# Delta-rule order, output projection and weight splits of a diffusion backbone: four edits in one change

## The reference

```
def odd_mixer(h_lat, h_ctx, ...):
    p = h @ w_in                      # q, k, v, z, a, b
    q, k, v = silu(short_conv(qkv));  q, k = l2_normalize(...)
    # per chunk: m = strict(kb k^T * decay); T = (I + m)^-1
    # u = T vb; w = T (kb exp(gcum))
    # scan over chunks, forward and backward: v_new = u - w S
    #   o = (q exp(g)) S + (q k^T * decay) v_new;  S = S exp(g_last) + ...
    o = rms_norm(o, norm_g) * silu(z)
    return o @ w_out                  # latent tokens only
```

## Time and profile before

| | |
|---|---|
| median of 3 runs | 1341.44 us (1340.7 to 1342.94) |
| profiled execution | 1340.64 us, span 1338.9 us |
| busy PE, DVE, ACT, POOL | 1200.1, 608.9, 567.1, 128.4 us |
| chain that ended last | PE 83%, DVE 6%, ACT 5%, issue 2%, DMA 2% |
| granted PE clock, mean | 0.947 of full |

### The profile page before, as it was taken

The page is one execution under the profiler, slowest core; times in us unless marked ns, Lnnn a source line. Parts: engine busy times, 40 slices in busy tenths (PEclk is TensorE's granted clock), DMA queues, the critical chain, the costliest instruction groups (busy, mean ns, idle before and its releaser), DMA issues.

```text
span 1338.9 us, 18940 instructions
## 1 busy us (share of the span) xinstructions
PE 1200.1 (90%) x7669; PEld 967.4 (72%) x7669; DVE 608.9 (45%) x948; ACT 567.1 (42%) x1028; POOL 128.4 (10%) x118
## 2 busy tenths in 40 slices
PE   5599999999889999999999698786988977999996
PEld 3377744457568888888887387664878967999996
DVE  2432247662543333332222663458756545554444
ACT  2432245663462223223222656253373636544442
POOL 0020320100001111110000000010015130111000
PEclk9699989999889999999999899887979987999998
DMA  8555558893223333333333032122203022666660
GB/s 287 181 166 164 172 178 299 279 264 83 63 63 95 95 95 96 101 97 88 99 89 97 16 95 53 42 63 68 75 2 96 1 77 81 189 187 178 176 184 33
DMA packets 239396, 159.62 MB, mean 119 GB/s; under 512 B 14779, under 2 KB 213837, under 8 KB 239309
## 3 DMA queue, kind: packets, MB, share of 16 engines
q1 hardware_dynamic: 238528, 158.11, 40.3%
q10 hardware_dynamic: 780, 0.29, 0.1%
HBM read 157.33 MB, written 1.05 MB: 118 GB/s over the span
## 4 chain that ended last, share of the span: by engine, by line
PE 83%; DVE 6%; ACT 5%; issue 2%; DMA 2%; POOL 1%; ACTq 0%; DVEq 0%; POOLq 0%
PE bank L1335 56%; PE bank L1373 4%; PE bank L1362 4%; PE bank L1322 3%; PE bank L1391 2%; PE bank L1484 2%; PE bank L1494 1%; PE bank L742 1%; PE bank L1515 1%; DVE v_conv L1070 1%; PE bank L745 1%; PE bank L1381 1%; PE bank L1510 1%; DMA alog_row<-in_gdn_a_log 1%; PE bank L699 1%
## 5 line engine op out<-in xcount | busy, mean ns | idle before, releaser
L1335 PE MATMUL bank<-h_hi,w_hi 128*128 128x512 f32 (+1 forms) x1048 | 374.4, 357 | 11.7 <-issue 11.7
L1335 PE MATMUL bank<-h_lo,w_hi 128*128 128x512 f32 (+1 forms) x1048 | 369.6, 353 | 0.0
L1335 PE MATMUL bank<-h_hi,w_lo 128*128 128x512 f32 (+1 forms) x1048 | 369.5, 353 | 0.0
L1781 DVE TENSOR_TENSOR w_lo<-w_raw,w_hi 128x1024 fp32r<-128x1024 f32 (+1 forms) x187 | 229.9, 1232 | 298.7 <-ACT w_hi L1577 298.5
L1577 ACT ACTIVATE w_hi<-w_raw 128x1024 fp32r<-128x1024 f32 (+1 forms) x187 | 192.7, 1036 | 98.4 <-PE bank L1335 82.3
L1335 PEld LDWEIGHTS bank<-h_hi,w_hi 128*128 128x128 f32 x1048 | 201.6, 192 | 39.5 <-issue 13.4
L1335 PEld LDWEIGHTS bank<-h_hi,w_lo 128*128 128x128 f32 x1048 | 201.3, 192 | 26.4
L1335 PEld LDWEIGHTS bank<-h_lo,w_hi 128*128 128x128 f32 x1048 | 201.3, 192 | 25.9 <-issue 0.5
L1335 PE MATMUL bank<-act_hi,w_hi 128*128 128x512 f32 (+1 forms) x352 | 118.3, 336 | 0.0
L1335 PE MATMUL bank<-act_lo,w_hi 128*128 128x512 f32 (+1 forms) x352 | 118.3, 336 | 0.0
L1335 PE MATMUL bank<-act_hi,w_lo 128*128 128x512 f32 (+1 forms) x352 | 118.3, 336 | 0.0
(11 more groups left out here) (260 smaller groups left out, 1448.6 us busy)
## 6 DMA issues: line engine op xcount, KB each, us to landing
w_raw<-in_ada_w SPq DMA_DIRECT2D x96, 512.0 KB, 5.2
w_raw<-in_ffn_w_gate_up SPq DMA_DIRECT2D x88, 512.0 KB, 3.8
w_raw<-in_ffn_w_down SPq DMA_DIRECT2D x32, 512.0 KB, 3.9
w_raw<-in_gdn_w_in SPq DMA_DIRECT2D x32, 512.0 KB, 4.0
w_raw<-in_attn_w_in SPq DMA_DIRECT2D x14, 512.0 KB, 4.0
w_raw<-in_ffn_w_down SPq DMA_DIRECT2D x16, 384.0 KB, 3.4
w_raw<-in_gdn_w_out SPq DMA_DIRECT2D x8, 512.0 KB, 5.4
w_raw<-in_attn_w_in SPq DMA_DIRECT2D x8, 256.0 KB, 3.5
```

What stands on the lines that cost most here:

```text
L1335: m = nc.tensor.matmul(dst, stationary(a, k), moving(b, k), start=(first and k == kk[0] and a == b == 0), stop=(last and k == kk[-1] and a ...
L1781: nc.vector.tensor_tensor(w_lo[where[key] % N_RAW][:, 0:tiles, 0:w], raw_slot(key)[:, 0:tiles, 0:w], w_hi[m % N_SPLIT][:, 0:tiles, 0:w].bi ...
```

## The change

1. Eight modulation chunks, not four, ahead of the first norm's sums.
2. Every norm: two weight tiles are split ahead of it, the third inside the loop over tiles, behind tile five.
3. The delta rule: decay banks 4 a step (before 3, 3, 4, 6); SiLU of k one step earlier; on DVE the Gram banks of the last step stand ahead of the taps of the tile; the second block transpose is moved behind `h_whole`; the 30 inversion steps lie evenly over steps 17 to 29, and the inverses leave one step later.
4. The output projection of the delta rule: plain fp32 with raw weights, the first three tiles interleaved over k; DVE gates and scales into `o_whole`. The splits and POOL's share are gone. Each read follows the O groups of its head half. The next feed-forward's three tiles are split during output tiles 5 to 7.

```diff
-ADA_FIRST = 4
+ADA_FIRST = 8
...
-        E_AT = {5: E_BANKS[0:3], 6: E_BANKS[3:6], 7: E_BANKS[6:10], 8: E_BANKS[10:16]}
+        E_AT = {5 + m: E_BANKS[4 * m:4 * m + 4] for m in range(4)}
...
+def split_out(split_to, i, m):
+    if i == 0:
+        split_to(ahead(("attout", m)))
+    elif m >= 5:
+        split_to(split_no[FIRST_CHUNK[3]] + m - 5)
...
-            jobs += scan_jobs(3, None, ("KS", "VN", "O"))
-            return jobs + [("read", pair) for pair in range(READS)]
+            jobs += scan_jobs(3, None, ("KS", "VN"))
+            for hq in range(2):
+                jobs += [("O", 3, d, hq) for d in range(2)] + [("read", 2 * hq + m) for m in range(2)]
+            return jobs
...
     for n in range(LAST + 1):        # gdn_vector
         if n < WHOLE_AT:
             split_to(ahead(("gdn",) + GDN_STEPS[n], LAST_SPLIT))
+        if n - 1 in G_AT:
+            gram_banks(n - 1)
...
-                if n == 15:
+                if n == 16:
                     link(blocks_out(1))
                     block_scale(1).then_inc(blocks_in, 1)
...
+            def project_gdn_out():
+                tiles = 3
+                dsts = [take(("y", 2, m))[:, CTX:T] for m in range(tiles)]
+                for m in range(tiles):
+                    wait_raw(pe, ("gdnout", m))
+                for k in range(KT):
+                    pe.wait_ge(o_whole_ready, k // 2 + 1)
+                    for m in range(tiles):
+                        ins = nc.tensor.matmul(dsts[m], raw_slot(("gdnout", m))[:, k, :], o_whole[:, k, :],
+                                               start=(k == 0), stop=(k == KT - 1))
...
             def pre_norm(i):         # DVE; ACT has the same behind its k == KT - 3
                 lo = first_token(i)
-                if i:
-                    split_to(ahead(FIRST_CHUNK[i]))
+                split_to(split_no[FIRST_CHUNK[i]] + 1)
...
+                        if m == KT - 4:
+                            split_to(ahead(FIRST_CHUNK[i]))
```

More of the change, by code:

```diff
@@ L377, in backbone @@
         where = {key: n for n, key in enumerate(chunks)}
-        split_chunks = [key for key in chunks if key[0] != "ada" and not (key[0] == "gdn" and key[1] in "qz")]
+        split_chunks = [key for key in chunks if key[0] != "ada" and key[0] != "gdnout"
+                        and not (key[0] == "gdn" and key[1] in "qz")]
         split_no = {key: n for n, key in enumerate(split_chunks)}
@@ L449, in backbone @@
         E_BANKS = [(c, d, hq) for c in range(CHUNKS) for d, hq in GROUPS]
-        E_AT = {5: E_BANKS[0:3], 6: E_BANKS[3:6], 7: E_BANKS[6:10], 8: E_BANKS[10:16]}
[L451 to L454, removed]
+        E_AT = {5 + m: E_BANKS[4 * m:4 * m + 4] for m in range(4)}
+        SOLVE_AT = {}
+        for m in range(13):
+            SOLVE_AT[17 + m] = [j for j in range(1, BLOCK - 1) if (j - 1) * 13 // 30 == m]
         VT_AT = {18 + m: [2 * m, 2 * m + 1] for m in range(GH // 2)}
@@ L1374, in project_whole @@
                 finish(m, key)
+            def project_gdn_out():
[8 more added lines that the diff above has]
+                                               start=(k == 0), stop=(k == KT - 1))
+                        if k == KT - 1:
+                            finish(ins, ("y", 2, m))
+                for m in range(tiles, KT):
+                    dst = take(("y", 2, m))[:, CTX:T]
+                    wait_raw(pe, ("gdnout", m))
+                    for k in range(KT):
+                        ins = nc.tensor.matmul(dst, raw_slot(("gdnout", m))[:, k, :], o_whole[:, k, :], start=(k == 0),
+                                               stop=(k == KT - 1))
+                    finish(ins, ("y", 2, m))
             def to_tokens(job, src, ring="work"):
@@ L1639, in out_project @@
                 for m in range(KT):
-                    split_to(ahead((name, m)))
+                    split_out(split_to, i, m)
                     take_y(i, m)
@@ L1893, in _ @@
             ada(ada_after("start", 0))
-            split_to(ahead(FIRST_CHUNK[0]))
             pre_norm(0)
@@ L1974, in _ @@
             for m in range(KT):
-                split_to(ahead(("attout", m)))
+                split_out(split_to, 0, m)
                 sum_y(0, m)
@@ L1984, in _ @@
                 for m in range(KT):
-                    split_to(ahead(("gdnout", m)))
+                    split_out(split_to, 2, m)
                     sum_y(2, m)
```

95 lines of the change are left out of this document (40 added, 55 removed).

## The result

The changed kernel takes 1300.19 us, the median of four runs (1297.48 to 1302.44), against 1342.19 for the kernel before beside it: a ratio of 0.9685, 95% interval 0.9661 to 0.9709, so 42.0 us less. Measured again later it had 0.9692 (0.9668 to 0.9717). The forecast was 1304.7 within 1298 to 1315. The profiled execution took 1299.38 us with a span of 1297.6 and a granted clock of 0.965, 41.3 us under that of before.

What follows compares the result with a forecast made beforehand. PE's long row of three-pass matmuls was taken as the floor, with gains only where it is broken: start -9.0, norms +0.1, delta rule to the join -21.9, scan and projection -5.9, sum -36.7, time 1304.7 us, range 1298 to 1315.

Steps and rivals of the forecast that it cites:

- The start: First projection: no hole in the load queue and no third tile ahead, so h_work begins at 42.9, not 51.92: -9.0 us.
- The third split: All norms: moved behind tile five it delays the last h_lo tiles, mostly hidden by PE's lag: +0.1 us, bounds 0 and +2.
- The delta rule's tiles: Delta rule up to h_whole: Gram multiplies run beside the tile; rebuilt stretch brings h_whole to 889.0 from 912.20: -23.2 us.
- The give-back at the join: End of q and z tiles: inverses leave a step later, giving back 1.3 us, bounds 0 and +4; -21.9 remains.
- the first still starts cold: First q tile behind h_whole: still begins on a low clock, 30 matmuls in 9.63 us at 0.50.
- rival (d): Q and z tiles: clock stays down, sixteen tiles and turns run at 1.2 GHz, +61 us, time 1365.7; chance 0.02.
- Scan and projection: End of scan: w_lo gone, projection starts 8.6 us sooner but costs 2.7 more: -5.9 us, bounds -3 and -7.
- My estimate of 33 us by that page: Output projection: fp32 counted as four passes, not three, turns 25.02 into some 33 us; gain nearly nothing, sum -31.
- The sum: Whole kernel: -9.0 + 0.1 - 21.9 - 5.9 = -36.7 us, giving 1304.7; chance of this forecast 0.65.
- (a): Start: loads 16 and 17 come after a queue hole, only the third tile's -3.8 is won, time 1309.9; chance 0.11.
- (b): Delta rule: DVE becomes the bound and the inverse slips by two tiles of 3.46, time 1311.6; chance 0.11.
- (c): Delta rule: Gram wait moved, not removed; one 4 us wait stays with 1.7 of cold clock, 1310.4; chance 0.08.

Runs made afterwards that it cites:

- both start edits: Kernel before with eight modulation chunks ahead of the first norm and the third split behind tile five of each norm: 1334.35 us, ratio 0.9947.
- the two dealings: Changed kernel with decay banks 4, 4, 4, 4 over steps 5 to 8 (1298.91 us, 0.9692) and with the old 3, 3, 4, 6 (1299.74 us, 0.9692).
- mask later: Kernel before with one added wait, so POOL masks the blocks only when h_whole is done: 1339.8 us, ratio 0.9993.
- norms late: Changed kernel with ACT's key norms at step 16 instead of 14: 1296.24 us, ratio 0.9666.
- the projection alone: Kernel before with the fp32 output projection and its read-outs (change 4) and none of the other changes: 1332.91 us, ratio 0.9945.

## Why the prediction was right, step by step

**The start** (-9.0): right as a sum, -8.97 in the profiled pair. Part of that is chance: the kernels without an edit here start anywhere from 54.0 to 56.1, and both edits together are worth some 8. The bound for the third tile alone (-3.8) measured -3.8 against their mean of 54.95. Inside the sum two terms were off and cancelled. The second weight tile's last byte came 2 us later than I had it in both kernels (ACT starts its split at 45.07 before, where I had 43.1, and at 40.44 after, where I had 38.5), and the work behind it is 2.5 to 3.0 us and not 4.4 to 5.0. What I had only as 0.6 us off that work is an edge of its own, the modulation: DVE finishes its fold at 40.68, and only then splits both tiles. The 38.2 that the Trainium skill's page "DMA: Bandwidth & Descriptors" would give was further off still from the 40.44.

**The third split** (+0.1, bounds 0 and +2): mis-sized. Norm 2 takes 36.4 us on the mean of seven traces with it (35.8 to 36.6) and 35.7 on the mean of seven without (35.2 to 36.5): +0.7, with ranges that overlap. The cover that I named, a PE that lags behind the tiles, was partly gone: in the changed kernel's chain of that norm ACT's split of the tile stands between `h_hi` and the next `h_work`:

```profile
753.03 0.95 ACT w_hi L1594
```

On the other side the stretch from the first projection to the attention's output is 248.1 to 248.6 in all but one of the eight traces with both start edits (250.3 in that one) and 249.5 to 250.2 in the other six: -1.2 on the means. I had not seen it, and its cause stays open; either edit alone does not give it (249.7 and 249.9).

**The delta rule's tiles** (-23.2): the rebuilt stretch hit. 142.0 became 118.8; `h_whole` starts at 879.43, which is 888.9 if the stretch begins where it did before, and I had 889.0; PE waited 4.6 of the 4.0 to 4.6. Counting waits alone (12.1 + 10.1) would have given 22 for the wrong reason, since a wait for `h_whole` of 4.6 stays. Within this stretch PE's idle time fell from 27.9 us to 8.0, and its busy time by 3.3. PE from the first Gram pair to the first q tile (length, busy, clock), before and then now:

```profile
836.86:912.70 75.84, 52.95 (x233) 0.87 0.20 53
```

```profile
829.80:880.00 50.20, 45.55 (x233) 1.00 0.33 84
```

The same instructions were busy for 7.4 us less there, at the higher clock. Ahead of it the busy time rose by 4.1, as much as the 3 x 2.04 - 1.99 of the sum. The +2.4 that is left of it behind the waits is what the two dealings show.

**The give-back at the join** (+1.3): this step failed, since the stretch got 2.2 us shorter. The longer line on DVE is there: from the first 32 q and z matmuls to the last turned transpose it is 68.3 us for 67.2, so +1.0. But two things that I had not priced outweigh it. POOL's mask no longer stops `h_whole` (-2.5, from the kernel with the mask later), and the first q tiles are less cold (-0.7):

```profile
880.00:888.83 8.83, 8.83 (x34) 0.81 0.23 60
```

A clock of 0.81 over the first 32 matmuls, where the kernel before had 0.66 (0.50 in its first 8.2 us) and the kernel with the mask later, which has no second wait there, 0.75. They take 9.51 us behind a wait of 8.95 (mask later), 8.83 behind 4.65 (changed) and 7.14, at 1.00, behind 1.64 (norms late). My sentence "the first still starts cold" was too strong, and rival (d), which built on it, was far off.

**Scan and projection** (-5.9): right in the number, and partly by luck. The -5.9 was meant at the projection's end. There the changed kernel is 4.4 us ahead of before, counted from the last turned transpose (the projection alone 5.3); another 1.6 came from the norm behind, on a warmer clock, which I had not forecast. The last VN ended 1.6 sooner where I had 2.7, and from there to the projection it took 15.9 where I had 15.3. The fp32 projection took 27.64 us for the 27.7 forecast. Here the Trainium skill's rule (page "FP8 and Floating Point Precision", section "TensorE Precision Notes") deserves more than I gave it. A weight tile took 3.46 us, against 2.72 for half of a warm three-pass tile of 5.44, a ratio of 1.27 and not far from the 4 to 3 of the rule. My estimate of 33 us by that page was wrong because I scaled 25.02, which holds cold matmuls; scaled from 2.72 it is 29.0. The projection itself costs 2.6 us more than before; the gain lies in its start, 7.1 us sooner. How much of that the missing splits give and how much the order of reads and tiles was not separated.

**The sum** (-36.7) missed 4.6 of the 41.3 us in the profiled pair: 3.5 at the join, 1.8 between the first projection and the first long row, less 1.1 for norm 2; the rest is within 0.4, with the two errors in the last term set off against each other. The rivals (a), (b) and (c) did not come: no hole, no lag of DVE, no Gram wait.

## What to carry to other kernels

Where an engine's wait repeats in every step, rebuild the stretch from the lines that will stand there and their durations; don't subtract the waits. Before looking for a better plan, look at what stands directly ahead of the operation that everyone waits for: here two small activations cost TensorE 3.0 us in the traces and a mask of 2.5 us on another engine cost it 2.5, while the block transpose, the decay banks and the SiLU together gave 1.3. And compare traces by stages: a microsecond or two in one stage of one trace may be the clock's, and a second trace of the same kernel tells.

## What the runs showed of the hardware

**DVE's two-input instructions stand still beside a mask on POOL.** In the kernel before, eight adds beside a 2.49 us mask on POOL took 4.91 us instead of 2.77; with the mask moved, the taps beside it 4.29 instead of 2.3. In the changed kernel the mask runs from 888.25 and it is one small multiply that waits:

```profile
888.48 2.20 DVE L1098 TENSOR_TENSOR gates<-gates,key_sums 128x64 f32<-128x64 f32 x1
```

It took 0.22 in the kernel with the mask later. In these three cases DVE loses 2.0 to 2.1 us, most of the mask's length (2.4 to 2.8), be its own work eight adds, three taps or one small multiply. The multiply ends at 890.68 and the mask at 890.62. The reciprocal just ahead of it, with one input, overlaps the mask for 0.2 us and took 0.35 us, as it did in the kernel with the mask later. The Trainium skill's page "SBUF — State Buffer", section "Who interferes with whom", says why: a VectorE instruction with two SBUF inputs contends with a GpSimd instruction that reads SBUF for a shared pair of ports, and that pair is an exclusive lock. The trace agrees, and by this rule I could have priced it.

**The clock's dips move.** The same 24 matmuls of a tile take 5.5 to 5.7 us or 6.9 to 7.3 (8.43 once) with no wait inside; in the first trace of the changed kernel their durations step from 0.63 to 0.39 us within one tile. The cold tile is the second, the sixth, both or none, and in one trace the second, fourth and fifth, also where no edit is near:

```profile
775.12:782.03 6.91, 6.91 (x26) 0.80 0.07 22
```

```profile
774.13:779.67 5.54, 5.54 (x27) 1.00 0.14 43
```

Here it is 0.80 in one trace of the changed kernel and 1.00 in the other. What sets the place of a dip was not found out.
